# The split tokens and hidden tiles of the experts, stored as interleaved pairs of high and low part

## The chip, the cores and the metric

One core of a Trainium2 chip runs the whole program. The metric is the device time of one execution in microseconds. Five engines work side by side and meet at semaphores: TensorE (PE; its loads of stationary tiles are listed as PEld), VectorE (DVE), ScalarE (ACT), GpSimd (POOL) and SyncE (SP), which issues nearly all transfers.

## The reference, cut to what matters

A bidirectional encoder trunk of two layers on 256 tokens of width 1024. Each layer has four parallel mixers, a gated sum of them, a feed-forward part and a gated embedding. In layer 0 the feed-forward part is one dense SwiGLU; in layer 1 it is a top-2-of-8 mixture of SwiGLU experts of width 3584, and this is what the change touches:

```python
def swiglu(x, w1, w3, w2):
    return (jax.nn.silu(x @ w1) * (x @ w3)) @ w2

def moe_swiglu(x, router, w1, w3, w2):
    logits = jnp.einsum('bsd,de->bse', x, router, preferred_element_type=jnp.float32)
    top_val, top_idx = lax.top_k(logits, TOP_K)
    top_w = jax.nn.softmax(top_val, axis=-1)
    combine = ...                       # (tokens, experts), two entries per token
    for e in range(N_EXPERTS):
        out = out + combine[..., e:e + 1] * swiglu(x, w1[e], w3[e], w2[e])
    return out
```

All inputs and the output are 32-bit floats.

## The kernel before, in words

**Split products.** A product of 32-bit operands is made of three matmuls on operands of type float32r: each operand is stored as a high part (a copy rounded to that type) and a low part (operand minus high part), and `three` (L895 to L899) adds high x high (L897), high x low (L898) and low x high (L899). Its first argument pair holds the stationary tiles, 128 x 128 numbers that are loaded into TensorE before the matmul, and the second pair the moving ones, which stream through it. Every matmul has its own load. In the profile a matmul is written `ps<-moving,stationary`.

**The expert stage.** Each expert is one pass over at most 128 of its tokens (up to 16 passes by the router's counts; 8 here). A pass has 14 chunks of 256 hidden columns. ScalarE makes the high part of each weight unit (`whi`, 128 x 1024, L1563), VectorE the low part (`wlo`, L2128), from a ring of six blocks of 1024 KB that SyncE fills; a chunk takes three blocks, six units. TensorE's chunk is, in order (`step`, L1110):

- 24 up products for the next chunk (`up_unit`, L1079): for each of the 8 slices k of the width, the token tile `xhi`/`xlo[:, k, 0:128]` is stationary and 512 weight columns (w1 and w3 together) move, into one PSUM bank.
- after half of these, two transposes of the present chunk's hidden tile (L1121), which ScalarE copies as high part (`hhi`, L1642) and VectorE turns into the low part (`hlo`, L2277).
- 12 down products (L1137): the hidden tile's two halves `hhi`/`hlo[:, parity, half, 0:128]` are stationary, 512 columns of w2 move.

In chunks 1 to 4 of a pass two scatter products each (L1092) bring the previous pass's results back to the tokens; in chunk 12 the next pass's tokens are gathered (L1073), and ScalarE (L1614) and VectorE (L2254) write them as `xhi` and `xlo`. The order of instructions on every engine is written out by hand. The waits around the changed tiles: TensorE's down products wait for `s_hl`, its up products of a new pass for `s_xl`; ScalarE's writes wait for the transposes and gathers, VectorE's for ScalarE's.

**Where the tiles lie.** `xhi` and `xlo` are 8 x 256 numbers per partition, of which the experts use the first 128 of each 256; `hhi` and `hlo` are 2 x 2 x 256, used likewise. They serve the dense layer and the mixers too, with all 256. In a partition the tensors `xhi`, `xlo`, `hhi`, `hlo`, `whi`, `wlo`, `ring_lo` and `query_key_high_x` start at a multiple of 128 bytes, and so do all their 128-number tiles. `query_key_high` starts 64 bytes past such a multiple.

**Three other places that are spoken of.** In `project` the products `token_major` (L626) have token tiles as stationary operand and 256 weight columns moving; for its last four blocks (`by_parity`) the tile is every second token, `xhi[:, k, tt:256:2]`, so its numbers are 8 bytes apart and start 0 or 4 bytes past the multiple; the first 24 of them have tt = 0 and the next 24 tt = 1. In `query_key` (L670) the stationary tiles are weights: the high part, used for two of the three matmuls, lies in `query_key_high` for the first blocks and then in `query_key_high_x`, the low part in `ring_lo`; 256 tokens move. L1490 on ScalarE copies 128 numbers per partition out of PSUM to every second element of `ybr`, backwards (a step of -2); L1250 copies 256 to neighbouring elements.

Of the kernel before, what the change touches and what calls it, by code (L numbers as in the profile page):

```python
# [29 lines left out]
P = 128  # L30
# [109 lines left out]
AK = SEQ + 2 * P  # L140
BK = TT * SEQ + 2 * P
LINE = 16
DUALS = HP * TT
HEAD_ROWS = ATT_GROUPS * 2 * SEQ


def trunk_program(nc, x, wm, wd, we, wp, pk_in, cst_in, onehot, relb, out):

    ctx = ExitStack()
    with ctx:  # L150
        def sb(name, shape, dt=F32):
            return ctx.enter_context(nc.sbuf_tensor(name, shape, dt))
# [111 lines left out]
        comb = sb("comb", [P, TT, MAX_PASSES + 1])  # L264
        msk = sb("msk", [P, TT, N_EXPERTS])
        pos = sb("pos", [P, TT, MAX_PASSES + 1])


        n_oh = ATT_GROUPS * 2 * SEQ
# [7 lines left out]
        def bank(b, lo=0, n=512):  # L277
            return ps[:, 512 * b + lo:512 * b + lo + n]
# [278 lines left out]
        def _(pe):  # L557
# [343 lines left out]
            def both(hi, lo, *at):  # L901
                return hi[at], lo[at]
# [161 lines left out]
            def experts(passes):  # L1064
# [14 lines left out]
                def up_unit(cc, u, slot, units):  # L1079

                    pe.wait_ge(s_wl, units + (u + 1))
                    for k in (2 * u, 2 * u + 1):
                        col = (k % 2) * 512
                        m = three(bank(cc % 2), both(xhi, xlo, slice(None), k, slice(0, P)),
                                  both(whi, wlo, slice(None), (slot + u) % SLOTS, slice(col, col + 512)),
                                  k == 0, k == KT - 1)
                    m.then_inc(s_wu, 1)
# [18 lines left out]
                with pe.Fori(0, n_p) as q:  # L1106
# [3 lines left out]
                    def step(k, cc, between=None):  # L1110

                        units = u0 + k * 6
                        pe.wait_ge(s_hm, c0 + k)
                        for u in range(4):
                            if cc == EXP_CHUNKS - 1 and u % 2 == 0:
                                pe.wait_ge(s_xl, q * 2 + (6 + u // 2 + 1))
                            up_unit(cc + 1, u, 4, units)
                            if u == 1:
                                pe.wait_ge(s_hm, c0 + k + 1)
                                for half in range(2):  # L1120
                                    m = pe.transpose(bank(2 + cc % 2, half * P, P), gt[:, 0, half * P:half * P + P],  # L1121
                                                     con("ident"))
                                m.then_inc(s_ht, 1)
                        if cc == EXP_CHUNKS - 2:
                            pe.wait_ge(s_stc, q + 2)
                            gather(q + 1)
                        if cc == 0:
                            pe.wait_ge(s_edc, q + 1)
                        if k is cc and 1 <= k <= 4:
                            pe.wait_ge(s_stc, q + 1)  # L1130
                            scatter(q, 2 * k - 2)
                            scatter(q, 2 * k - 1)
                        pe.wait_ge(s_hl, c0 + k + 1)
                        for half in range(2):
                            pe.wait_ge(s_wl, units + (5 + half))
                            for col in range(0, D_MODEL, 512):
                                m = three(bank(4 + col // 512), both(hhi, hlo, slice(None), cc % 2, half, slice(0, P)),  # L1137
                                          both(whi, wlo, slice(None), 2 + half, slice(col, col + 512)),
                                          cc == 0 and half == 0, cc == EXP_CHUNKS - 1 and half == 1)
                            m.then_inc(s_wu, 1)  # L1140
# [81 lines left out]
        def _(act):  # L1222
# [383 lines left out]
            def experts():  # L1606
# [3 lines left out]
                def tokens(n):  # L1610

                    for j in range(2):
                        act.wait_ge(s_xg, n * 2 + (j + 1))
                        act.activation(xhi[:, 4 * j:4 * j + 4, 0:P], bank(6 + j).rearrange("p (c t) -> p c t", c=4),  # L1614
                                       ACT.Copy).then_inc(s_xgc, 1)

                def sums(n):
# [9 lines left out]
                with act.Fori(0, n_p) as q:  # L1627
# [4 lines left out]
                    def chunk(k, cc, j, rr):  # L1632
# [5 lines left out]
                        if cc == EXP_CHUNKS - 2:  # L1638
                            act.wait_ge(s_st, q + 1)
                            act.activation(sca[:, :], bank(6, 0, SEQ), ACT.Copy).then_inc(s_stc, 1)  # L1640
                        act.wait_ge(s_ht, c0 + k + (1 - DENSE_CHUNKS))
                        act.activation(hhi[:, cc % 2, :, 0:P], bank(2 + cc % 2, 0, SEQ).rearrange(  # L1642
                            "p (h t) -> p h t", h=2), ACT.Copy).then_inc(s_hh, 1)
                        if cc == 0:
                            sums(q)
# [80 lines left out]
        def _(dve):  # L1726
# [519 lines left out]
            def experts():  # L2246
# [3 lines left out]
                def tokens(n):  # L2250

                    for j in range(2):
                        dve.wait_ge(s_xgc, n * 2 + (j + 1))
                        dve.tensor_tensor(xlo[:, 4 * j:4 * j + 4, 0:P], bank(6 + j).rearrange("p (c t) -> p c t", c=4),  # L2254
                                          xhi[:, 4 * j:4 * j + 4, 0:P], ALU.subtract).then_inc(s_xl, 1)

                def add(n, m_):

# [9 lines left out]
                with dve.Fori(0, n_p) as q:  # L2268
# [3 lines left out]
                    def chunk(k, cc, j):  # L2272
# [1 line left out]
                        dve.tensor_tensor(hid[:, 0, :], hs[:, 0, :], bank(cc % 2, SEQ, SEQ), ALU.mult).then_inc(s_hm, 1)  # L2274
                        lows(u0 + (k * 6 + 4), 2, 2, j)
                        dve.wait_ge(s_hh, c0 + k + 1)
                        dve.tensor_tensor(hlo[:, cc % 2, :, 0:P], bank(2 + cc % 2, 0, SEQ).rearrange(  # L2277
                            "p (h t) -> p h t", h=2), hhi[:, cc % 2, :, 0:P], ALU.subtract).then_inc(s_hl, 1)
                        if cc == EXP_CHUNKS - 2:
                            dve.wait_ge(s_st, q + 1)  # L2280
                            slots_of(q + 1)
# [282 lines left out]
```

## Time and profile before

| | us |
|---|---|
| three runs | 2147.4, 2148.34, 2148.71 (median 2148.34) |
| the profiled execution, its own time | 2148.84 |
| its span, first to last instruction | 2146.8 |
| TensorE busy | 2116.5 |
| VectorE busy | 1684.4 |
| ScalarE busy | 1323.6 |
| expert loop, from its first to its last chunk (1087.4 to 2092.7) | 1005.3 |

Busy time of TensorE counts overlapping matmuls once, and the end of a matmul is modelled, so what one matmul costs in a stream is read from the distance between starts. A span holds only instructions; the time of an execution is about 2 us more.

### The profile page before, as it was taken

Reading aid. Unit: us, or ns where it says so; the run is one execution under the profiler, and the core shown is the slowest. Engines: PE = TensorE matmul, PEld = TensorE weight load, DVE = VectorE, ACT = ScalarE, POOL = GpSimd, SP = SyncE. Lnnn points to the kernel's source line nnn. Section 1 sums busy time; section 2 is a strip of 40 time slices with the busy share of each in tenths; the row PEclk is TensorE's granted clock in tenths of the full one; section 3 lists DMA queues with packets and bytes.
Section 4 is the critical chain, followed back from the end, with each engine's and each line's share of the span. In section 5 each row is a group of like instructions: output and inputs, shape, how many; then the busy total and the mean of one; then the engine's idle time right before and its main releaser. Section 6 shows DMA issues by size and latency. Waiting matters only on the chain.

```text
span 2146.8 us, 37284 instructions
## 1 busy us (share of the span) xinstructions
PE 2116.5 (99%) x13622; PEld 1905.2 (89%) x13622; DVE 1684.4 (78%) x2373; ACT 1323.6 (62%) x1864; POOL 24.3 (1%) x45
## 2 busy tenths in 40 slices
PE   9999999999999999999999999999999999999997
PEld 8999999999999999999888888888888888888886
DVE  4998866655456898766688888998989899898985
ACT  5545654454435446654467777777777777777773
POOL 0000100000000000100000000000000000000000
PEclk9999999999999999999999999999999999999998
DMA  7534436355345434435379898898999989899981
GB/s 253 188 118 154 143 142 236 138 196 176 137 158 182 164 113 169 147 132 223 138 282 364 341 350 347 345 374 328 358 350 349 347 345 369 339 361 341 351 310 76
DMA packets 74965, 533.19 MB, mean 248 GB/s; under 512 B 8655, under 2 KB 8655, under 8 KB 11000
## 3 DMA queue, kind: packets, MB, share of 16 engines
q1 hardware_dynamic: 72620, 525.04, 64.6%
q0 software_dynamic: 2048, 6.29, 1.6%
q8 instruction: 68, 1.11, 0.2%
q10 hardware_dynamic: 204, 0.54, 0.1%
q14 instruction: 25, 0.20, 0.0%
HBM read 530.74 MB, written 1.10 MB: 248 GB/s over the span
## 4 chain that ended last, share of the span: by engine, by line
PE 95%; DVE 3%; ACT 1%; DMA 1%; issue 0%; SPq 0%; DVEq 0%; ACTq 0%
PE ps L897 28%; PE ps L899 28%; PE ps L898 28%; PE ps L560 4%; PE ps L1092 1%; PE ps L1121 1%; PE ps L851 1%; PE ps L879 1%; PE ps L763 1%; PE ps L866 1%; DMA constants_sb<-constants 0%; DVE rstd L1736 0%; DVE wlo L2128 0%; PE ps L572 0%; DVE xn L1742 0%; DMA ring<-w_ple 0%
## 5 line engine op out<-in xcount | busy, mean ns | idle before, releaser
L2128 DVE TENSOR_TENSOR wlo<-ring,whi 128x1024 fp32r<-128x1024 f32 x746 | 872.8, 1220 | 145.6 <-ACT whi L1563 143.9
L1563 ACT ACTIVATE whi<-ring 128x1024 fp32r<-128x1024 f32 x746 | 749.1, 1054 | 137.9 <-PE ps L899 131.7
L897 PE MATMUL ps<-whi,xhi 128*128 128x512 f32 (+1 forms) x1160 | 434.7, 375 | 1.5 <-DVE xlo L2254 1.5
L899 PE MATMUL ps<-whi,xlo 128*128 128x512 f32 (+1 forms) x1160 | 426.8, 368 | 0.0
L898 PE MATMUL ps<-wlo,xhi 128*128 128x512 f32 x904 | 352.9, 390 | 0.0
L897 PE MATMUL ps<-xhi,whi 128*128 128x256 f32 x960 | 276.6, 288 | 2.5 <-DVE gt L2150 1.4
L898 PE MATMUL ps<-xlo,whi 128*128 128x256 f32 x960 | 273.4, 285 | 0.0
L899 PE MATMUL ps<-xhi,ring_lo 128*128 128x256 f32 x896 | 254.2, 284 | 0.0
L899 PEld LDWEIGHTS ps<-whi,xlo 128*128 128x128 f32 x1160 | 219.2, 189 | 35.8
L897 PEld LDWEIGHTS ps<-whi,xhi 128*128 128x128 f32 x1160 | 219.6, 189 | 33.6 <-DVE xlo L2254 1.9
L899 PE MATMUL ps<-xhi,wlo 128*128 128x256 f32 x704 | 199.2, 283 | 0.0
L898 PEld LDWEIGHTS ps<-wlo,xhi 128*128 128x128 f32 x904 | 170.2, 188 | 32.1
L897 PEld LDWEIGHTS ps<-xhi,whi 128*128 128x128 f32 x960 | 186.1, 194 | 4.7 <-DVE gt L2150 1.6
L898 PEld LDWEIGHTS ps<-xlo,whi 128*128 128x128 f32 x960 | 186.0, 194 | 0.3
L897 PE MATMUL ps<-whi,hhi 128*128 128x512 f32 x448 | 182.7, 408 | 0.0
L899 PE MATMUL ps<-whi,hlo 128*128 128x512 f32 x448 | 175.0, 391 | 0.0
L898 PE MATMUL ps<-wlo,hhi 128*128 128x512 f32 x448 | 174.5, 390 | 0.0
L899 PEld LDWEIGHTS ps<-xhi,ring_lo 128*128 128x128 f32 x896 | 172.4, 192 | 0.0
L1642 ACT ACTIVATE hhi<-ps 128x256 fp32r<-128x256 f32 x112 | 43.0, 384 | 187.9 <-PE ps L1121 187.9
L899 PEld LDWEIGHTS ps<-xhi,wlo 128*128 128x128 f32 x704 | 135.0, 192 | 0.0
L1750 DVE TENSOR_TENSOR ring_lo<-ring,whi 128x1024 fp32r<-128x1024 f32 x68 | 79.8, 1220 | 41.1 <-ACT whi L1242 30.2
L1453 ACT ACTIVATE gs<-ps,half_b_gate 128x256 f32<-128x256 f32 x64 | 30.2, 472 | 122.6 <-PE ps L899 122.6
(307 smaller groups left out, 3832.5 us busy)
## 6 DMA issues: line engine op xcount, KB each, us to landing
ring<-w_experts SPq DMA_DIRECT2D x340, 1024.0 KB, 5.4
ring<-w_mixers SPq DMA_DIRECT2D x114, 1024.0 KB, 4.9
ring<-w_dense SPq DMA_DIRECT2D x33, 1024.0 KB, 4.8
ring<-w_ple SPq DMA_DIRECT2D x10, 1024.0 KB, 4.9
bias<-bias_rows POOLq DMA_DIRECT2D x8, 256.0 KB, 7.1
cvfa<-bias_rows POOLq DMA_DIRECT2D x8, 256.0 KB, 5.2
constants_sb<-constants SPq DMA_DIRECT2D x1, 1048.0 KB, 9.1
h<-x_in SPq DMA_DIRECT2D x1, 1024.0 KB, 4.8
```

What stands on the lines that cost most here:

```text
L560: m = pe.matmul(dst, a, b, start=k == 0, stop=k == len(lhs) - 1)
L763: m = pe.matmul(bank(g, part * P, P), dta[:, tt, at:at + 1].to_broadcast([P, P]), con("from" if d else "upto"), start=True, stop=True)
L851: m = pe.matmul(bank(4 + u, at, n), qk[64 * u:64 * u + 64, g, i, tt * P:tt * P + P], qk[64 * u:64 * u + 64, ATT_GROUPS + g, i, key:key + n ...
L866: m = pe.transpose(bank(u, b * P, P), sa[:, u, b * P:b * P + P], con("ident"))
L897: pe.matmul(dst, lhs[0], rhs[0], start=first, stop=False, skip_group_check=True)
L898: pe.matmul(dst, lhs[0], rhs[1], start=False, stop=False, skip_group_check=True)
L899: return pe.matmul(dst, lhs[1], rhs[0], start=False, stop=last, skip_group_check=True)
L1453: act.activation(gs[:, m_ % 2, :], bank(first_bank + m_ % banks, SEQ, SEQ), ACT.Tanh, bias=half_b[:, bass.ds(b * KT + m_, 1)], scale=0.5). ...
L1563: act.activation(whi[:, slot, :], ring[:, j % RING, lo:lo + UNIT], ACT.Copy).then_inc(s_wh, 1)
L1642: act.activation(hhi[:, cc % 2, :, 0:P], bank(2 + cc % 2, 0, SEQ).rearrange("p (h t) -> p h t", h=2), ACT.Copy).then_inc(s_hh, 1)
L1750: dve.tensor_tensor(ring_lo[:, j % RING, cols], ring[:, j % RING, cols], whi[:, (2 * j + u) % SLOTS, :], ALU.subtract).then_inc(s_ed, 1)
L2128: dve.tensor_tensor(wlo[:, slot, :], ring[:, j % RING, lo:lo + UNIT], whi[:, slot, :], ALU.subtract).then_inc(s_wl, 1)
```

## The change

Two new buffers hold the experts' operands. `x_pair` has, for each slice k, 256 numbers in which high and low part of one token alternate, and 4 more that stay empty, so slices are 1040 bytes apart. `h_pair` is the same for the hidden tiles, with 8 empty numbers after each 256, 1056 bytes apart. Both buffers start at a multiple of 128 bytes. A stationary tile is now every second number, 8 bytes apart; the tiles of x start 0, 16, 32, ... 112 bytes past a multiple of 128, those of h 0, 32, 64 and 96, and the low part of each 4 bytes further. ScalarE and VectorE write with the same step, in the same instructions as before. `xhi`, `xlo`, `hhi` and `hlo` remain for the rest of the program, and the new buffers lie behind all others, so no other address changes. On every engine the order, number and waits of instructions are the same. Lines behind L142 move down by one, those behind L266 by 19.

```diff
--- before.py
+++ after.py
@@ -140,6 +140,7 @@
 AK = SEQ + 2 * P
 BK = TT * SEQ + 2 * P
 LINE = 16
+XSTEP, HSTEP = 4, 8
 DUALS = HP * TT
 HEAD_ROWS = ATT_GROUPS * 2 * SEQ
 
@@ -264,6 +265,24 @@
         comb = sb("comb", [P, TT, MAX_PASSES + 1])
         msk = sb("msk", [P, TT, N_EXPERTS])
         pos = sb("pos", [P, TT, MAX_PASSES + 1])
+        x_pair = sb("x_pair", [P, KT, 2 * P + XSTEP], F32R)
+        h_pair = sb("h_pair", [P, 2, 2, 2 * P + HSTEP], F32R)
+
+        def x_part(part, first, n):
+
+            return x_pair[:, first:first + n, 0:2 * P].rearrange("p c (t s) -> p s c t", s=2)[:, part]
+
+        def x_tile(k):
+
+            return x_part(0, k, 1)[:, 0], x_part(1, k, 1)[:, 0]
+
+        def h_part(part, par_):
+
+            return h_pair[:, par_, :, 0:2 * P].rearrange("p h (t s) -> p s h t", s=2)[:, part]
+
+        def h_tile(par_, half):
+
+            return h_part(0, par_)[:, half], h_part(1, par_)[:, half]
 
 
         n_oh = ATT_GROUPS * 2 * SEQ
@@ -1081,7 +1100,7 @@
                     pe.wait_ge(s_wl, units + (u + 1))
                     for k in (2 * u, 2 * u + 1):
                         col = (k % 2) * 512
-                        m = three(bank(cc % 2), both(xhi, xlo, slice(None), k, slice(0, P)),
+                        m = three(bank(cc % 2), x_tile(k),
                                   both(whi, wlo, slice(None), (slot + u) % SLOTS, slice(col, col + 512)),
                                   k == 0, k == KT - 1)
                     m.then_inc(s_wu, 1)
@@ -1134,7 +1153,7 @@
                         for half in range(2):
                             pe.wait_ge(s_wl, units + (5 + half))
                             for col in range(0, D_MODEL, 512):
-                                m = three(bank(4 + col // 512), both(hhi, hlo, slice(None), cc % 2, half, slice(0, P)),
+                                m = three(bank(4 + col // 512), h_tile(cc % 2, half),
                                           both(whi, wlo, slice(None), 2 + half, slice(col, col + 512)),
                                           cc == 0 and half == 0, cc == EXP_CHUNKS - 1 and half == 1)
                             m.then_inc(s_wu, 1)
@@ -1611,7 +1630,7 @@
 
                     for j in range(2):
                         act.wait_ge(s_xg, n * 2 + (j + 1))
-                        act.activation(xhi[:, 4 * j:4 * j + 4, 0:P], bank(6 + j).rearrange("p (c t) -> p c t", c=4),
+                        act.activation(x_part(0, 4 * j, 4), bank(6 + j).rearrange("p (c t) -> p c t", c=4),
                                        ACT.Copy).then_inc(s_xgc, 1)
 
                 def sums(n):
@@ -1639,7 +1658,7 @@
                             act.wait_ge(s_st, q + 1)
                             act.activation(sca[:, :], bank(6, 0, SEQ), ACT.Copy).then_inc(s_stc, 1)
                         act.wait_ge(s_ht, c0 + k + (1 - DENSE_CHUNKS))
-                        act.activation(hhi[:, cc % 2, :, 0:P], bank(2 + cc % 2, 0, SEQ).rearrange(
+                        act.activation(h_part(0, cc % 2), bank(2 + cc % 2, 0, SEQ).rearrange(
                             "p (h t) -> p h t", h=2), ACT.Copy).then_inc(s_hh, 1)
                         if cc == 0:
                             sums(q)
@@ -2251,8 +2270,8 @@
 
                     for j in range(2):
                         dve.wait_ge(s_xgc, n * 2 + (j + 1))
-                        dve.tensor_tensor(xlo[:, 4 * j:4 * j + 4, 0:P], bank(6 + j).rearrange("p (c t) -> p c t", c=4),
-                                          xhi[:, 4 * j:4 * j + 4, 0:P], ALU.subtract).then_inc(s_xl, 1)
+                        dve.tensor_tensor(x_part(1, 4 * j, 4), bank(6 + j).rearrange("p (c t) -> p c t", c=4),
+                                          x_part(0, 4 * j, 4), ALU.subtract).then_inc(s_xl, 1)
 
                 def add(n, m_):
 
@@ -2274,8 +2293,8 @@
                         dve.tensor_tensor(hid[:, 0, :], hs[:, 0, :], bank(cc % 2, SEQ, SEQ), ALU.mult).then_inc(s_hm, 1)
                         lows(u0 + (k * 6 + 4), 2, 2, j)
                         dve.wait_ge(s_hh, c0 + k + 1)
-                        dve.tensor_tensor(hlo[:, cc % 2, :, 0:P], bank(2 + cc % 2, 0, SEQ).rearrange(
-                            "p (h t) -> p h t", h=2), hhi[:, cc % 2, :, 0:P], ALU.subtract).then_inc(s_hl, 1)
+                        dve.tensor_tensor(h_part(1, cc % 2), bank(2 + cc % 2, 0, SEQ).rearrange(
+                            "p (h t) -> p h t", h=2), h_part(0, cc % 2), ALU.subtract).then_inc(s_hl, 1)
                         if cc == EXP_CHUNKS - 2:
                             dve.wait_ge(s_st, q + 1)
                             slots_of(q + 1)
```

## Rows read from the trace of the kernel before

**Rows 1.** The page's first part: busy us (share of the span), instructions.
```profile
PE 2116.5 (99%) x13622; PEld 1905.2 (89%) x13622; DVE 1684.4 (78%) x2373; ACT 1323.6 (62%) x1864; POOL 24.3 (1%) x45
```
**Rows 2.** The chain that ended last: shares by engine, and by line.
```profile
PE 95%; DVE 3%; ACT 1%; DMA 1%; issue 0%; SPq 0%; DVEq 0%; ACTq 0%
PE ps L897 28%; PE ps L899 28%; PE ps L898 28%; PE ps L560 4%; PE ps L1092 1%; PE ps L1121 1%; PE ps L851 1%; PE ps L879 1%; PE ps L763 1%; PE ps L866 1%; DMA constants_sb<-constants 0%; DVE rstd L1736 0%; DVE wlo L2128 0%; PE ps L572 0%; DVE xn L1742 0%; DMA ring<-w_ple 0%
```
**Rows 3.** Window of the expert loop: busy us by engine, clock, DMA share, GB/s.
```profile
1087.40:2092.70 1005.30, 1005.30 (x4657) 829.98 (x4655) 895.18 (x1008) 755.25 (x936) 0.00 (x0) 1.00 0.91 348
```
**Rows 4.** Order of time, TensorE, one plain chunk: start us, length us, instruction.
```profile
1533.05 0.39 PE L897 MATMUL ps<-whi,hhi 128*128 128x512 f32 x1
...
1538.26 0.40 PE L899 MATMUL ps<-whi,xlo 128*128 128x512 f32 x1
1538.50 0.38 PE L1121 MATMUL ps<-constants_sb,gt 128*128 128x128 f32 x2
...
1538.95 0.39 PE L898 MATMUL ps<-wlo,xhi 128*128 128x512 f32 x1
...
1540.11 0.39 PE L897 MATMUL ps<-whi,xhi 128*128 128x512 f32 x1
...
1541.47 0.39 PE L897 MATMUL ps<-whi,hhi 128*128 128x512 f32 x1
```
**Rows 5.** TensorE's groups by form: count, busy us, mean ns, idle us before.
```profile
L897 PE MATMUL ps<-whi,xhi 128*128 128x512 f32 x904 | 362.3, 401 | 1.5 <-DVE xlo L2254 1.5
L898 PE MATMUL ps<-wlo,xhi 128*128 128x512 f32 x904 | 352.9, 390 | 0.0
...
L897 PE MATMUL ps<-whi,hhi 128*128 128x512 f32 x448 | 182.7, 408 | 0.0
```
**Rows 6.** Order of time, TensorE, value products of layer 0 with every second token.
```profile
102.44 0.28 PE L897 MATMUL ps<-whi,xhi 128*128 128x256 f32 x1
...
105.32 0.28 PE L897 MATMUL ps<-whi,xhi 128*128 128x256 f32 x1
...
108.20 0.28 PE L897 MATMUL ps<-whi,xhi 128*128 128x256 f32 x1
```
**Rows 7.** Order of time, TensorE, query and key products of layer 0.
```profile
143.37 0.28 PE L897 MATMUL ps<-xhi,query_key_high 128*128 128x256 f32 x1
...
153.26 0.28 PE L897 MATMUL ps<-xhi,query_key_high_x 128*128 128x256 f32 x1
...
156.14 0.33 PE L560 MATMUL ps<-ybr,mm 128*128 128x64 f32 x2
```
**Rows 8.** ScalarE's instructions on ybr, then on L1614: ns min/median/max.
```profile
L1250 ACT ACTIVATE ybr<-ps x16: 384/384/388, 67.2 to 731.4; 128x256 f32<-128x256 f32 x16
L1490 ACT ACTIVATE ybr<-ps x16: 275/293/295, 251.4 to 964.0; 128x128 f32<-128x128 f32 x16
...
L1614 ACT ACTIVATE xhi<-ps x18: 576/597/602, 1078.5 to 2081.9; 128x512 fp32r<-128x512 f32 x18
```
**Rows 9.** Order of time, VectorE, a plain chunk; in brackets the wait before.
```profile
1530.91 0.43 DVE L2277 TENSOR_TENSOR hlo<-ps,hhi 128x256 fp32r<-128x256 f32 x1 [0.24 <-ACT hhi L1642]
1531.86 4.63 DVE L2128 TENSOR_TENSOR wlo<-ring,whi 128x1024 fp32r<-128x1024 f32 x4 [0.52 <-ACT whi L1563]
```
**Rows 10.** Order of time, VectorE and TensorE, a pass's new tokens.
```profile
1579.15 1.34 DVE L2254 TENSOR_TENSOR xlo<-ps,xhi 128x512 fp32r<-128x512 f32 x2
...
1581.73 0.39 PE L897 MATMUL ps<-whi,xhi 128*128 128x512 f32 x1
```
**Rows 11.** A ten-microsecond window (columns as rows 3), and the ring's transfers.
```profile
1600.00:1610.00 10.00, 10.00 (x46) 8.25 (x45) 10.00 (x13) 7.70 (x10) 0.00 (x0) 1.00 0.98 402
...
ring<-w_experts SPq DMA_DIRECT2D x340, 1024.0 KB, 5.4
```

## The prediction

> **What bounds the kernel now.** I read the page's first part, then the chain that ended last, then the windows, the groups by form, and last the order of time. TensorE is busy 2116.5 us of 2146.8, VectorE 1684.4 [rows 1]. The chain lies on TensorE for 95% of the span, and 84% of the span is three lines, L897 to L899, the three products of split operands in `three` [rows 2]. The window of the expert loop is the stage that the change touches: 1005.3 us, TensorE busy in all of it, granted clock 1.00 (the upper level, 2.4 GHz), DMA engines 0.91 [rows 3]. So what is left to win there is the distance from one matmul's start to the next, and that stands in the order of time. A plain chunk, from one first down product to the next, is 1541.47 - 1533.05 = 8.42 us. In it 23 undisturbed steps take 1538.26 - 1533.05 = 5.21 us, and the last six 1541.47 - 1540.11 = 1.36 us: 226.7 ns each [rows 4]. The 512 columns alone need 512 / 2.4 = 213.3 ns, so 13.3 ns of each step are not columns.
>
> **How many steps can change.** The loaded (stationary) tiles of the token products are xhi and xlo, of the down products hhi and hlo; each stands in three lines with 904 and 448 matmuls at 512 columns [rows 5]: 3 x 904 + 3 x 448 = 4056. No instruction is added, removed or moved; no semaphore changes; no other buffer's address changes. What changes is where in a partition the 128 loaded numbers lie: before, neighbours, each tile at a multiple of 128 bytes; after, every second number, x tiles at 0, 16, ... 112 bytes past such a multiple (low parts 4 bytes further), h tiles at 0, 32, 64, 96.
>
> **What place costs: the trace has both parts, each at 256 columns.** Step two by itself: the value products take every second token of xhi and xlo as loaded tile, at 0 and 4 bytes past a multiple of 128. The 24 matmuls with tiles at 0 bytes run from 102.44 to 105.32, the 24 with tiles at 4 bytes from there to 108.20 [rows 6]: 2.88 us each, 120.0 ns a step. With neighbouring numbers at multiples of 128 the step is the same: the query and key products that load from query_key_high_x take 156.14 - 153.26 = 2.88 us for 24 [rows 7]. So step two at these places costs and gives nothing. Place by itself: the same routine a moment earlier loads from query_key_high, 64 bytes past a multiple of 128, for two of its three products; the third loads from ring_lo, at a multiple. 84 of them take 153.26 - 143.37 = 9.89 us, 117.7 ns [rows 7]. That is 2.3 ns less per matmul, or 2.3 / (2/3) = 3.4 ns for each tile that lies off the multiple. So while one matmul streams, the load of the next tile slows it, by an amount that hangs on where the two lie.
>
> A rule speaks against this. The Trainium skill ("TensorE: Matmul & The Clock Gate", section "Step-by-step: what each phase is for") says that "Loading the next tile's weights doesn't steal SBUF read bandwidth from the running matmul". By that rule a tile's place cannot change the step, and the change would be worth nothing. The 117.7 beside 120.0 ns [rows 7] doesn't agree with it, at least at 256 columns.
>
> **The sum.** Tiles off a multiple of 128 after the change: x 7 of 8, 2712 x 7/8 = 2373; h 3 of 4 (counting the 4-byte shift as none, since it gave 120.0 above), 1344 x 3/4 = 1008; together 3381. At -3.4 ns: -11.5 us. From both sides the price of one such tile is unknown at 512 columns: at best all 13.3 ns go, at worst the step is the one seen when matmul and load have lost their rhythm. After the two transposes of each chunk the next steps are longer: five take 1540.11 - 1538.95 = 1.16 us, 232 ns, 5.3 over the steady 226.7 [rows 4]. So -13.3 to +5.3 ns a tile, -45 to +18 us. I take -3.4 ns, from the row that is nearest in what it varies, the loaded tile's place; the two ends stay for the range.
>
> The writers of the new tiles: ScalarE and VectorE write every second element, 112 chunks and 9 gathers of tokens. ScalarE's writes with a step of -2 in the trace, 128 elements, took 293 ns against 384 for 256 neighbours [rows 8]; at (597 - 384) / 256 = 0.83 ns an element, from the 512-element copy of tokens [rows 8], 128 neighbours would be 277. So 0 to 16 ns more per 128 elements, and for VectorE, where no row shows it, from nothing to twice the time. Neither is on the chain: the low part of a chunk's hidden tile is ready at 1530.91 + 0.43 = 1531.34 [rows 9], and the first product that it stands in starts after 1533.05 [rows 4], 1.7 us later. Doubled, both engines' writes would take 0.8 us more, still covered. The tightest place is the new tokens of a pass: VectorE done at 1579.15 + 1.34 = 1580.49, TensorE's first product with them at 1581.73 [rows 10], 1.24 us. Doubled writes of both engines would eat that and cost some 0.1 us in each of 8 passes, 1 us. I put 0.
>
> Who is next if TensorE gains: VectorE has 0.24 + 0.52 us of waiting in a plain chunk of 8.42 [rows 9], so it needs 7.66; a chunk without any collision would be 8.42 - 36 x 0.83 x 0.0133 = 8.02. The ring brings three blocks of 1024 KB per chunk, 392 GB/s at 8.02 us; ten-microsecond stretches reach 402 [rows 11], and the loop's mean would rise only from 348 [rows 3] to 364. Neither stops a gain of this size.
>
> The execution that the profile shows took 2148.84 us: a span of 2146.8 and 2.0 around it; the median of the three runs is 2148.34, the same within 0.03%. 2148.8 - 11.5 = 2137.3. Forecast 2137 us.
>
> **Rivals.**
> 1. Nothing changes. A load with step two walks twice as many bytes while it runs, and the only stretch with it shows 120.0 ns at both places tried; if place matters only for neighbours, the step stays 226.7. For it: 120.0 ns with step two [rows 6]. Against: those tiles lie within 4 bytes of the multiple, where place gives nothing either. Time: 2149. The quoted rule gives the same.
> 2. Slower: the rhythm is lost. At 512 columns the steady 226.7 ns is the shortest step that lasts, reached only after five longer ones each time [rows 4]. If tiles that lie differently from one product to the next keep throwing load and stream out of that rhythm, each of the 3381 costs 5.3 ns more: +18 us, 2167. For it: it is the only row of lost rhythm at 512 columns. Against: at 256 columns a changing place made the mean step shorter, not longer. It decides as soon as the mean step in the loop passes 226.7.
> 3. The collision goes wholly. If load and stream only hold each other up where they are at the same place of a 128-byte span at the same time, a load that starts elsewhere with step two may never be: -45 us, 2104. For it: 13.3 of 226.7 ns is there to take, and no other engine stops it. Against: the 117.7 of place alone is still far from the 106.7 ns that 256 columns need.
>
> **Chances.** A change under 0.2% (4.3 us) can't be told from none here. The forecast, a gain of 4 to 25 us, 0.42; rival 3, more than that, 0.16; rival 1 0.17; rival 2 0.25. So faster 0.58, same 0.17, slower 0.25. The range reaches to both bounds, since cases of both signs stand against each other: 2106 to 2168; the forecast's own is 2124 to 2144.
>
> **What would show it.** Right: in the expert loop the steady step falls below 226.7 ns and varies with the tile, a plain chunk is near 8.32 us, and the loop is shorter by the whole gain, with everything before it as it was. The hidden tile's writes stay near 0.38 and 0.43 us, and VectorE's waits shrink. Wrong: steps of 227 throughout (rival 1); steps of 230 and more in the whole chunk, not just after the transposes (rival 2); steps near 214 to 216 (rival 3); or VectorE's subtraction far above 0.43 us with TensorE waiting for it, which would make the writes the price.

## The result, and the profile after

| | before | after |
|---|---|---|
| median of the runs, us | 2148.53 (4 runs) | 2166.45 (4 runs, 2165.41 to 2167.29) |
| ratio after / before | | 1.0084, 95% interval 1.0067 to 1.0102 |
| profiled execution, us | 2148.84 | 2165.41 |
| first to last of the 4056 products of the experts, us | 1081.85 to 2092.65: 1010.80 | 1080.21 to 2108.22: 1028.01 |
| plain chunk, median of 71, us | 8.42 | 8.60 |

The change makes the kernel 0.8% slower. The forecast was 2137 us, faster; what came is the time of rival 2 (2167), at the upper edge of the range.

The page's first part of the kernel after answers to [rows 1], the chain by engine and line to [rows 2] (L916 to L918 are the old L897 to L899):

```profile
PE 2133.3 (99%) x13622; PEld 1932.9 (89%) x13622; DVE 1684.9 (78%) x2373; ACT 1324.7 (61%) x1864; POOL 24.3 (1%) x45
...
PE 95%; DVE 3%; ACT 1%; DMA 1%; issue 0%; SPq 0%; DVEq 0%; ACTq 0%
```

The window from the first to the last product of the experts, in the kernel after and then in the kernel before (us; busy us of PE, PEld, DVE, ACT, POOL; granted clock; DMA share; GB/s):

```profile
1080.21:2108.22 1028.01, 1028.01 (x4679) 862.87 (x4680) 898.59 (x1011) 758.44 (x938) 0.00 (x0) 1.00 0.88 341
```
```profile
1081.85:2092.65 1010.80, 1010.80 (x4679) 834.60 (x4680) 898.12 (x1011) 757.37 (x938) 0.00 (x0) 1.00 0.91 347
```

The same instructions, the same clock, VectorE and ScalarE busy within 1.1 us of before. TensorE is busy all the time and takes 17.21 us longer. Only PE and its loads (PEld, +28 us) have grown. The whole difference therefore lies in the time from one of TensorE's starts to the next. Here is the order of time of one plain chunk after, to be held against [rows 4]:

```profile
1530.40 0.40 PE L916 MATMUL ps<-whi,h_pair 128*128 128x512 f32 x1
...
1533.20 0.39 PE L916 MATMUL ps<-whi,x_pair 128*128 128x512 f32 x1
...
1535.75 0.39 PE L918 MATMUL ps<-whi,x_pair 128*128 128x512 f32 x1
1535.98 0.38 PE L1140 MATMUL ps<-constants_sb,gt 128*128 128x128 f32 x2
...
1536.44 0.39 PE L917 MATMUL ps<-wlo,x_pair 128*128 128x512 f32 x1
...
1538.99 0.39 PE L916 MATMUL ps<-whi,h_pair 128*128 128x512 f32 x1
```

The 12 down products take 1533.20 - 1530.40 = 2.80 us, 233 ns each; the 12 up products after them 1535.98 - 1533.20 = 2.78, 232 ns; the last 11 1538.99 - 1536.44 = 2.55, 232 ns. The settled 226.7 ns of [rows 4] are gone (1% of the token products' steps in the stage last 226 or 227 ns, 75% before); in the plain chunk before, 232 ns were only the five steps behind the transposes. Over the whole stage, taking the times from start to start of neighbouring products of 512 columns: 2431 token products went from a mean of 227.9 to 232.4 ns (+10.8 us), 1287 products of hidden tiles from 228.2 to 233.4 (+6.7). Together 17.5 us, against 17.9 between the medians. The groups by form tell the same [rows 5]: what grew is the modelled length of every product, and the loads beside them (195 ns of one, 188 before; run 2 below has 195 too, runs 3 and 6 have 188 to 189 and lose as much, so the loss does not need the longer load). TensorE's idle time before the new tokens' products, 1.7 us, hardly moved.

```profile
L916 PE MATMUL ps<-whi,x_pair 128*128 128x512 f32 x904 | 366.8, 406 | 1.7 <-DVE x_pair L2273 1.7
L917 PE MATMUL ps<-wlo,x_pair 128*128 128x512 f32 x904 | 355.7, 393 | 0.0
L916 PE MATMUL ps<-whi,h_pair 128*128 128x512 f32 x448 | 185.1, 413 | 0.0
```

The writes are as forecast. ScalarE's copy of a hidden tile takes 402 ns, VectorE's low part the 425 ns it took before, and TensorE waits for neither:

```profile
L1661 ACT ACTIVATE h_pair<-ps 128x256 fp32r<-128x256 f32 x112 | 45.0, 402 | 194.5 <-PE ps L1140 194.5
L2296 DVE TENSOR_TENSOR h_pair<-ps,h_pair 128x256 fp32r<-128x256 f32 x112 | 47.6, 425 | 54.0 <-ACT h_pair L1661 54.0
```

### The profile page after: what moved, and what is told of

Same layout as the page of the kernel before. It is cut to its first block, busy times and chain, and to the rows that moved or that the text cites. A ratio compares the mean times of both kernels' runs of the same rounds, so it can differ in the third digit from the quotient of the medians.

```text
span 2163.3 us, 37284 instructions
## 1 busy us (share of the span) xinstructions
PE 2133.3 (99%) x13622; PEld 1932.9 (89%) x13622; DVE 1684.9 (78%) x2373; ACT 1324.7 (61%) x1864; POOL 24.3 (1%) x45
## 4 chain that ended last, share of the span: by engine, by line
PE 95%; DVE 3%; ACT 1%; DMA 1%; issue 0%; SPq 0%; DVEq 0%; ACTq 0%
PE ps L916 28%; PE ps L918 28%; PE ps L917 28%; PE ps L579 4%; PE ps L1111 1%; PE ps L1140 1%; PE ps L870 1%; PE ps L898 1%; PE ps L782 1%; PE ps L885 1%; DMA constants_sb<-constants 0%; DVE rstd L1755 0%; DVE wlo L2147 0%; PE ps L591 0%; DVE xn L1761 0%; DMA ring<-w_ple 0%
## 5 line engine op out<-in xcount | busy, mean ns | idle before, releaser
L916 PE MATMUL ps<-whi,x_pair 128*128 128x512 f32 x904 | 366.8, 406 | 1.7 <-DVE x_pair L2273 1.7
L918 PE MATMUL ps<-whi,x_pair 128*128 128x512 f32 x904 | 357.7, 396 | 0.0
L917 PE MATMUL ps<-wlo,x_pair 128*128 128x512 f32 x904 | 355.7, 393 | 0.0
L916 PE MATMUL ps<-xhi,whi 128*128 128x256 f32 x960 | 276.0, 288 | 2.6 <-DVE gt L2169 1.4
L918 PE MATMUL ps<-xhi,ring_lo 128*128 128x256 f32 x896 | 253.9, 283 | 0.0
L918 PEld LDWEIGHTS ps<-whi,x_pair 128*128 128x128 f32 x904 | 175.9, 195 | 33.6
L916 PEld LDWEIGHTS ps<-whi,x_pair 128*128 128x128 f32 x904 | 175.8, 194 | 31.7 <-DVE x_pair L2273 2.1
L917 PEld LDWEIGHTS ps<-wlo,x_pair 128*128 128x128 f32 x904 | 176.1, 195 | 31.0
L918 PE MATMUL ps<-xhi,wlo 128*128 128x256 f32 x704 | 199.2, 283 | 0.0
L916 PEld LDWEIGHTS ps<-xhi,whi 128*128 128x128 f32 x960 | 185.6, 193 | 4.7 <-DVE gt L2169 1.6
L916 PE MATMUL ps<-whi,h_pair 128*128 128x512 f32 x448 | 185.1, 413 | 0.0
L917 PE MATMUL ps<-wlo,h_pair 128*128 128x512 f32 x448 | 177.2, 396 | 0.0
L918 PE MATMUL ps<-whi,h_pair 128*128 128x512 f32 x448 | 176.6, 394 | 0.0
L918 PEld LDWEIGHTS ps<-xhi,ring_lo 128*128 128x128 f32 x896 | 171.8, 192 | 0.0
L1661 ACT ACTIVATE h_pair<-ps 128x256 fp32r<-128x256 f32 x112 | 45.0, 402 | 194.5 <-PE ps L1140 194.5
L918 PEld LDWEIGHTS ps<-xhi,wlo 128*128 128x128 f32 x704 | 135.0, 192 | 0.0
```

Source lines behind the costliest of these rows:

```text
L916: pe.matmul(dst, lhs[0], rhs[0], start=first, stop=False, skip_group_check=True)
L917: pe.matmul(dst, lhs[0], rhs[1], start=False, stop=False, skip_group_check=True)
L918: return pe.matmul(dst, lhs[1], rhs[0], start=False, stop=last, skip_group_check=True)
L1661: act.activation(h_part(0, cc % 2), bank(2 + cc % 2, 0, SEQ).rearrange("p (h t) -> p h t", h=2), ACT.Copy).then_inc(s_hh, 1)
```

## The experiments

In the quoted expectations theories A and B of run 1 hold for runs 1 to 3, run 4 names its own, and those of run 8 (R, P, H) hold for runs 9 to 11. "Step one" means neighbouring numbers, "step two" every second one. Runs 1, 4 and 8 are benches of TensorE alone and compute nothing of the reference; the others compute all of it.

**1. Each place alone, on TensorE.** Blocks of 60 matmuls with one load each, from tiles at a set place, 24 to settle and 36 measured.

> Leaves out the whole network: TensorE alone runs 66 blocks of 60 matmuls, each block with one pattern of where the loaded tile and the moving columns lie (step one or two; 0, 16, ... 112 bytes past a multiple of 128), at 512 and at 256 columns; the first 24 of a block settle, the step is read from the last 36. Theory A (the step depends on whether the place changes from one load to the next, not on step two): one place throughout gives 226.7 ns at 512 columns and 120.0 at 256, whatever the place and with step one or two alike; changing places (the eight of the changed kernel, or 64, 64, 0) give 230 to 236 ns at 512 and 117 to 119 at 256. Theory B (step two itself costs at 512 columns): step two gives about 232.6 ns at every place, the eight places with step one stay at 226.7.

Order of time of the bench (one row per block; the first two are 36 measured steps with the tile at 0 bytes and the next block's first 24, the last two the same at 32 bytes):

```profile
19.18 8.32 PE L78 MATMUL ps<-stream_at0b,load_step1at0b 128*128 128x512 f32 x36
27.34 5.60 PE L75 MATMUL ps<-stream_at0b,load_step1at16b 128*128 128x512 f32 x24
...
46.55 8.56 PE L78 MATMUL ps<-stream_at0b,load_step1at32b 128*128 128x512 f32 x36
54.95 5.76 PE L75 MATMUL ps<-stream_at0b,load_step1at48b 128*128 128x512 f32 x24
```

From start to start the place 0 takes (27.34 - 19.18) / 36 = 226.7 ns, the place 32 (54.95 - 46.55) / 36 = 233.3. No other engine works here, so the dearer step needs neither DMA nor writes. At 512 columns nothing is below 226.7; only places 0 and 16 with step one reach it, the rest lie between 229.0 and 234.3, step two at every place between 230.0 and 233.4. At 256 columns the order turns round: 120.0 at place 0, 116.7 to 118.8 at most others. The forecast had carried the sign of 256 columns over to 512.

**2 and 3. Half of the change each.** Run 2 keeps the pairs and drops the empty numbers, so that all tiles start at one place; run 3 keeps the places and stores high and low apart.

```diff
-XSTEP, HSTEP = 4, 8
+XSTEP, HSTEP = 0, 0
```
```diff
-        x_pair = sb("x_pair", [P, KT, 2 * P + XSTEP], F32R)
+        x_pair = sb("x_pair", [P, 2, KT, P + XSTEP], F32R)
...
-            return x_pair[:, first:first + n, 0:2 * P].rearrange("p c (t s) -> p s c t", s=2)[:, part]
+            return x_pair[:, part, first:first + n, 0:P]
```

> The changed kernel without the 4 and 8 empty numbers: pairs with step two, all tiles at 0 or 4 bytes past a multiple of 128. Theory A (changing places cost): steps of 226.7 ns again and 2148 to 2150 us, ratio 1.000. Theory B (step two costs): steps near 232.6 ns and 2166 us, ratio 1.008. Theory C (the writes with step two cost): TensorE waits for x_pair or h_pair, also 2166 us.

> The other half of the change: high and low parts apart, neighbouring numbers (step one), the x tiles at the eight places 0, 16, ... 112 and the h tiles at 0, 32, 64, 96 bytes past a multiple of 128. Theory A: steps of 230 to 236 ns, about 2166 us, ratio 1.008. Theory B: 226.7 ns and 2148 us, ratio 1.000.

Run 2: 2166.03 us, 1.0082 (1.0065 to 1.0098). Run 3: 2165.11, 1.0075 (1.0059 to 1.0092). Each half alone costs all of it. The halves do not add up; each is enough to take away the settled 226.7 ns (means of 233.3 and 233.0 ns for tokens and hidden tiles in run 2, 233.2 and 231.9 in run 3).

**4. Widths.** The bench again, with widths between 192 and 512 columns and some finer places.

> TensorE alone, as in the first bench (each matmul has its own load; 24 to settle, 36 measured): widths of 192, 256, 320, 384, 448 and 512 columns, each with the loaded tile's numbers neighbours at 0, 16, 32 and 64 bytes past a multiple of 128, and every second number at 0; then streams at 16 and 48, and tiles at 4, 8 and 12 bytes, at 256 and 512 columns. The first bench had 120.0, 118.3, 120.1, 117.8 and 120.0 ns at 256 columns and 226.7, 226.7, 233.4, 229.0 and 231.4 at 512. Theory A (the sign belongs to the width: the load's reads fit beside short streams and break the rhythm of long ones): the price of a place moves steadily from -2 to +2 or more ns between 256 and 512, crossing zero near 384 columns. Theory B (the 512-column step at place 0 is one lucky fit): at 320, 384 and 448 columns the places off the multiple are as cheap as place 0 or cheaper, within 1 ns, and 512 alone stands out.

| ns per step, columns | place 0 | 16 | 32 | 64 | step two, 0 |
|---|---|---|---|---|---|
| 192 | 111.6 | 111.7 | 111.7 | 111.7 | 120.1 |
| 256 | 120.0 | 118.2 | 119.9 | 117.7 | 121.2 |
| 320 | 146.7 | 146.7 | 146.7 | 146.7 | 148.0 |
| 384 | 173.3 | 173.3 | 176.7 | 173.3 | 175.0 |
| 448 | 202.7 | 206.7 | 205.3 | 199.9 | 205.0 |
| 512 | 226.7 | 226.7 | 233.4 | 228.8 | 231.4 |

Neither theory as written: no steady drift with the width, and 512 is not a single exception. The price hangs on width and place together. The finer places at 512 columns have a tile 4 bytes past a multiple that costs no more than the one at 0:

```profile
401.14 8.32 PE L72 MATMUL ps<-stream_at0b,load_step1at4b 128*128 128x512 f32 x36
409.30 5.70 PE L69 MATMUL ps<-stream_at0b,load_step1at8b 128*128 128x512 f32 x24
```

(409.30 - 401.14) / 36 = 226.7 ns at 4 bytes; the trace has 230.7 at 8 and 233.3 at 12. At the end of this bench the block of 256 columns at place 64 came a second time, behind another block, and took 113.3 ns instead of 117.7: at one address two rhythms can last.

**5 and 6. One place for all tiles, in the kernel.**

```diff
+PLACE = 4
...
+            at = PLACE + (part * KT + first) * P
+            return x_pair[:, at:at + n * P].rearrange("p (c t) -> p c t", t=P)
```

PLACE counts numbers of 4 bytes: 4 in run 5 (16 bytes), 8 in run 6 (32 bytes); hidden tiles likewise.

> The kernel before with the experts' tiles in buffers of their own, high and low apart, neighbouring numbers, and all tiles 16 bytes past a multiple of 128. If the time follows the bench's price of the place (226.7 ns at 512 columns, as at the multiple): 2148.5 us, 2146 to 2151. If any place off the multiple breaks the rhythm of 512 columns: about 2165 us, as the eight places did.

> The same with all tiles 32 bytes past the multiple. By the bench's price, 233.4 ns, +6.7 ns for 4056 matmuls: +27 us, 2175 us (2171 to 2179), the slowest of all so far. If all places off the multiple cost alike: 2165 to 2166 us, as the eight places (2165.11) and the pairs (2166.03) did. If the tile's place were not the cause, and the new buffers alone were: also 2165.

Place 16: 2162.97 us, 1.0067 (1.0051 to 1.0082). Place 32: 2166.58, 1.0086 (1.0071 to 1.0102). The bench's price of the place failed for 16 bytes (2148.5 was expected from it) and was too high for 32. So "bytes past a multiple of 128" did not look like the right variable.

**7. A version meant to win.** The experts' tiles in buffers of their own at multiples of 128, and `xhi`, `xlo`, `hhi`, `hlo` as a whole 64 bytes further, for the 256-column products that stream them.

```diff
+        pad_a = sb("pad_a", [P, LINE])
         xhi = sb("xhi", [P, KT, SEQ], F32R)
         xlo = sb("xlo", [P, KT, SEQ], F32R)
+        pad_b = sb("pad_b", [P, LINE])
```

> A version that may beat both. The experts' tiles lie in buffers of their own at multiples of 128, neighbouring numbers (226.7 ns at 512 columns); xhi, xlo, hhi and hlo, which the 256-column products of the mixers, the dense layer and the embeddings stream, move as a whole to 64 bytes past a multiple. The bench has 117.8 ns for a load at 0 and a stream at 64, against 120.0 at 0 and 0. Some 5136 such steps x -2.2 = -11.3 us, 384 loads of tokens at 64 another -0.8, 512 query and key steps +0.5 (118.7 against 117.7): -11.6, so 2137 us (2134 to 2142). If place at 256 columns were no gain in the kernel, or these stages wait for weights rather than for TensorE: 2148 to 2150.

2140.01 us, 0.9965 (0.9955 to 0.9976): a gain, but of another make than expected. In the profiled execution, the fastest of eight (2135.03 to 2145.24), the experts began 22.0 us earlier (1059.85), and their stage became 10.7 us longer (1021.46). Order of time of a plain chunk there:

```profile
1533.35 0.39 PE L924 MATMUL ps<-whi,h_pair 128*128 128x512 f32 x1
...
1535.38 0.40 PE L924 MATMUL ps<-whi,h_pair 128*128 128x512 f32 x1
1535.62 0.40 PE L922 MATMUL ps<-whi,x_pair 128*128 128x512 f32 x1
...
1538.41 0.38 PE L1146 MATMUL ps<-constants_sb,gt 128*128 128x128 f32 x2
```

Hidden tiles: nine steps in 2.03 us, 226 ns, the settled rhythm. Token tiles: twelve in 2.79 us, 232 ns, though they too start at a multiple of 128. What may tell the two apart is the distance in bytes from the loaded tile to the stream. By the addresses that the program gives them, `x_pair` lies 128 bytes (mod 256) from `whi` and `wlo`, `h_pair` 0. In the kernel before both were 0.

**8. The distance, measured.** One load buffer and one stream; the distance set in steps of 32 bytes, each block behind 8 matmuls of 128 columns ("free") or behind these and 20 settled steps at distance 0 ("led").

> TensorE alone. In the streams64 run the experts' token tiles stood at multiples of 128 and yet took 232 ns, the hidden tiles 227; token tiles were 384 bytes (mod 512) from the streams, hidden tiles 0; in the kernel before 256 and 0. So here load and stream lie a set distance apart, 0 to 992 bytes in steps of 32, at 512 columns, and 0 to 480 at 256; each block follows 8 matmuls of 128 columns ('free'), or those and then 20 steps at distance 0 ('led'). Theory R (the distance from load to stream counts, not the place past a multiple of 128): 226.7 at distances that are multiples of 256, 229 to 234 at all others, 128 and 384 included, and the same when both lie 128 further. Theory P (the place past a multiple of 128): 226.7 at every multiple of 128. Theory H (a rhythm that history sets): free and led differ, by 3 ns or more, at some of the same distances. Every second number: R 226.7 at 0 and 256; from the pairs that lay 256 apart and took 233, rather 231 or more at all distances.

Windows of 35 steps each (first column from:to, then the length), at 512 columns and a distance of 0, 128 and 256; then 0 and 128 again with load and stream both 128 bytes further; then at 256 columns distance 0, 64 free and 64 led:

```profile
16.77:24.70 7.93, 7.93 (x36) 6.57 (x35) 0.00 (x0) 0.00 (x0) 1.00 0.00 0
153.65:161.79 8.14, 8.14 (x37) 6.60 (x35) 0.00 (x0) 0.00 (x0) 1.00 0.00 0
290.37:298.31 7.94, 7.94 (x37) 6.57 (x35) 0.00 (x0) 0.00 (x0) 1.00 0.00 0
1111.14:1119.08 7.94, 7.94 (x37) 6.57 (x36) 0.00 (x0) 0.00 (x0) 1.00 0.00 0
1140.67:1148.80 8.13, 8.13 (x37) 6.59 (x35) 0.00 (x0) 0.00 (x0) 1.00 0.01 2
1466.07:1470.27 4.20, 4.20 (x38) 4.20 (x37) 0.00 (x0) 0.00 (x0) 1.00 0.00 0
1502.88:1506.85 3.97, 3.97 (x37) 3.97 (x36) 0.00 (x0) 0.00 (x0) 1.00 0.02 4
1513.07:1517.19 4.12, 4.12 (x37) 4.12 (x36) 0.00 (x0) 0.00 (x0) 1.00 0.00 0
```

35 steps in 7.93 or 7.94 us are 226.7 ns each at distances 0 and 256, in 8.13 or 8.14 us 232.4 at 128, and the same when both are moved by 128 bytes. The whole table, from the starts in the trace (load minus stream, mod 256; at 512 columns the four periods up to 992 agree within 0.2 ns):

| distance | 0 | 32 | 64 | 96 | 128 | 160 | 192 | 224 |
|---|---|---|---|---|---|---|---|---|
| 512 columns, step one | 226.7 | 233.3 | 233.3 | 234.3 | 232.4 | 233.3 | 229.0 | 233.3 |
| 512 columns, step two | 233.3 | | 230.0 | | 231.4 | | 233.3 | |
| 256 columns, free | 120.0 | 118.3 | 113.3 | 118.7 | 118.7 | 120.1 | 117.8 | 116.7 |
| 256 columns, led | 120.0 | 118.5 | 117.8 | 117.3 | 118.7 | 119.9 | 113.3 | 116.7 |

Theory R holds at 512 columns, in period and sign; place past a multiple of 128 does not. Of these distances history counts at 256 columns alone, at 64 and 192 (and by 1.4 ns at 96).

Read as distances, by the addresses of their buffers, benches 1 and 4 agree: there place 32 lies at distance 160, 64 at 192, 96 at 224, and step two at place 0 at 128. But between the steps of 32 bytes the price is not smooth. Distance 16 took 226.7 ns, 8 took 230.7 and 80 took 232.0, and the tile at 4 bytes of bench 4 lies at distance 132: 226.7, where 128 takes 232.4 and 140 takes 233.3. With load and stream both at place 16, distance 128 took 233.2. So 0 is the cheapest of the steps of 32, not the only cheap distance, and why the distance matters at all is not shown by any run.

**9 to 11. The distance in the kernel.** Run 9 is run 5 with PLACE = 0: tokens 0 bytes from the streams, hidden tiles 128. Run 10 is run 7 with the tokens' buffer moved by 128 bytes, to distance 0. Run 11 is run 9 with the hidden tiles' buffer moved likewise.

```diff
-        x_pair = sb("x_pair", [P, 2 * KT * P + 32], F32R)
+        pad_e = sb("pad_e", [P, 32])
+        x_pair = sb("x_pair", [P, 2 * KT * P], F32R)
```
```diff
+        pad_h = sb("pad_h", [P, 32])
         h_pair = sb("h_pair", [P, 8 * P + 32], F32R)
```

> The kernel before with the experts' tiles in the new buffers, high and low apart, neighbouring numbers, all at multiples of 128 bytes. Token tiles are then 256 (mod 512) from the streams as before, hidden tiles 384 instead of 0. Theory R: token steps 226.7, hidden steps near 232, +5 ns for 1287 steps: 2155 us (2152 to 2158). Theory P: both 226.7, 2148.5 us. If the new buffers by themselves were the cause: 2163 to 2166, both at 232.

> The streams64 version with its experts' token buffer moved by 128 bytes, so that token tiles are 0 (mod 512) from the streams, as hidden tiles were and are. Theory R: token steps fall from 232.5 to about 228, 2431 steps x -4.5 = -11 us from 2140: 2129 us (2125 to 2134). Theory P: nothing changes, 2140.

> The place0 version with its buffer for hidden tiles moved by 128 bytes, so that these too lie a multiple of 256 bytes from the streams; nothing else differs. Theory R, now with the bench's table (226.7 ns at distance 0 mod 256, 232.4 at 128, 229.0 at 192, 233 to 234 at 32, 64, 96, 160 and 224): hidden steps 233.0 back to 228, as in the kernel before, 1287 steps x -5 = -6.4 us, and the tokens' steps after them settle sooner, 2431 x -1.6 = -3.9: 2147 to 2149 us. Rival: the new buffers cost something by themselves, then it stays above 2152.

Run 9: 2157.57 us, 1.0042 (1.0027 to 1.0057). Run 10: 2129.49, 0.9918 (0.9905 to 0.9932). Run 11: 2148.63, 1.0003 (0.9994 to 1.0013). Each came where the distance put it. Runs 9 and 11 differ in nothing but 128 bytes of padding, and lie 9 us apart. Order of time of a plain chunk of run 9:

```profile
1535.74 0.40 PE L918 MATMUL ps<-whi,h_pair 128*128 128x512 f32 x1
...
1538.54 0.40 PE L918 MATMUL ps<-whi,x_pair 128*128 128x512 f32 x1
...
1540.15 0.39 PE L919 MATMUL ps<-wlo,x_pair 128*128 128x512 f32 x1
...
1541.06 0.40 PE L920 MATMUL ps<-whi,x_pair 128*128 128x512 f32 x1
```

Hidden tiles, distance 128: 2.80 / 12 = 233 ns. Token tiles, distance 0: seven steps in 1.61 us, 230 ns, while the rhythm settles, then four in 0.91, 227 ns. So a product at a bad distance also costs its followers at a good one: the token steps of this run average 229.5, and 227.9 again in run 11. Its window of all experts is that of the kernel before:

```profile
1081.73:2092.53 1010.80, 1010.78 (x4679) 834.60 (x4680) 898.06 (x1011) 757.33 (x938) 0.00 (x0) 1.00 0.92 347
```

Mean steps in the kernels beside the bench, for the distance of each (ns):

| | tokens: distance, bench, kernel | hidden tiles: distance, bench, kernel |
|---|---|---|
| before | 0, 226.7, 227.9 | 0, 226.7, 228.2 |
| run 2, step two | 0, 233.3, 233.3 | 0, 233.3, 233.0 |
| run 6 | 32, 233.3, 233.2 | 160, 233.3, 233.3 |
| run 7 | 128, 232.4, 232.5 | 0, 226.7, 228.8 |
| run 9 | 0, 226.7, 229.5 | 128, 232.4, 233.0 |
| run 11 | 0, 226.7, 227.9 | 0, 226.7, 228.2 |

One entry stays open: run 5 had its tokens at distance 16 and steps of 232.2, 15% of them at 226 or 227. Benches 1 and 4 have 226.7 there, behind a settled block; an unsettled entry at 16 alone was not tried. A block of bench 1 that alternates places 16 and 0 settled at 226.7 within three steps behind one at 231.7. So the distance alone does not foretell run 5.

**12. The best version.** Run 10 with the streams of the dense layer's second products, the low mixer weights and the low half of the mixed rows at distance 64 as well (moved by 128 bytes of padding behind `ring_lo`, and 192 before `mix_low`; the 64 bytes that run 10 has behind `mix_low` and the 128 before `x_pair` fall away, and the experts' tiles stay at distance 0).

```diff
         ring_lo = sb("ring_lo", [P, RING, BLK], F32R)
+        pad_r = sb("pad_r", [P, 2 * LINE])
...
+        pad_c = sb("pad_c", [P, 3 * LINE])
         mlo = sb("mix_low", [P, KT, SEQ], F32R)
```

> The streams64_near version with all 256-column products of the mixers' weights, the dense layer's second products and the low half of the mixed rows brought to a distance of 64 (mod 256) from load to stream, where the bench settled at 113.3 ns (or 117.8, by how it was entered); before, these stood at 192 (118 ns measured). 912 products of the dense hidden tiles 118.0 to 113.3: -4.2 us; 1056 with the low weights 118.5 to 117: -1.6: together 2123.5 us (2121 to 2127). If the other rhythm holds there (117.8): 2129, unchanged. The experts stay at 228.

2117.42 us (five executions, 2116.72 to 2127.96), 0.9874 (0.9856 to 0.9893): faster than both kernels, and 3.6 us below the lower end expected. The dense hidden tiles' products came to 113.3 ns (117.8 in run 10), as expected; 928 products with the low mixer weights did not gain (118.5 to 119.7 in the mean); and 736 products of `xhi` with `wlo`, whose distance was 64 in both, fell unasked from 116.9 to 113.7. Their neighbours' rhythm may have done it; no run shows that. The experts start at 1050.77, 31.1 us earlier than before, and their window is unchanged:

```profile
1050.77:2061.60 1010.83, 1010.83 (x4680) 834.50 (x4680) 898.18 (x1011) 757.38 (x938) 0.00 (x0) 1.00 0.92 347
```

The chain by engine, from the page of the same run: what lies on VectorE has grown from 3% to 7%. That is not yet a price: TensorE is idle for 31.7 us of the span (2114.9 less 2083.2 busy), 30.3 before.

```profile
PE 90%; DVE 7%; ACT 1%; DMA 1%; issue 0%; DVEq 0%; SPq 0%; ACTq 0%
```

## Why the prediction was wrong

**Which stage, how many steps, and where to look: right.** All of the loss lies in the 4056 products of the expert loop; the stretch before it is as it was, within 1.6 us. The 4056 steps, TensorE as the bound and the time between starts as the thing to read held.

**"What place costs": the step that failed.** The prediction took its price from 256 columns, -3.4 ns a tile, and gave it to tiles at 512. Two errors lay in it. First, the variable: [rows 7] was read as "64 bytes past a multiple of 128 against a multiple". By the addresses, `query_key_high` is 192 bytes (mod 256) from the stream `xhi`, `query_key_high_x` and `ring_lo` are 0. The first bench has the same mix at 256 columns, two loads at distance 192 and one at 0: 117.7 ns, and 120.0 for 0 alone, as the rows had it. (All loads at 192 take 117.8 there, so even at 256 columns the gain was not 3.4 ns for each tile off the multiple.) In the kernel before, these tiles and their streams that start at a multiple of 128 also lay 0 (mod 256) apart, so the two readings could not be told apart there. Second, the width: at 256 columns distance 0 is among the dearest states (120.0, others down to 113.3), at 512 nothing is cheaper (226.7, others to 234.3); that same mix of 192 and 0 takes 229.0 at 512. The term -11.5 us was in truth +17.5: not 3381 tiles at -3.4 ns, but nearly all products at +4.5 (tokens) and +5.2 (hidden tiles).

**"Step two costs and gives nothing": wrong at 512 columns.** [rows 6] has 120.0 ns at 256, and the first bench 118.3 to 122.2, but at 512 columns step two takes 230.0 to 233.4 at every distance tried, and run 2, with step two alone, cost the whole 17 us. Rival 1's condition failed here. The 4 bytes between high and low part, counted as none, changed nothing at step two (233.3 ns at distances 0 and 4), though with neighbouring numbers 4 bytes can matter (128 against 132). With TensorE alone at work the same matmul takes 226.7 or 232.4 ns by the loaded tile's distance: load and stream are not independent. The quoted rule of the Trainium skill ("TensorE: Matmul & The Clock Gate", section "Step-by-step: what each phase is for"), read as the prediction read it, allows no such difference; these runs do not agree with it.

**Rival 2 had the sign and the price, and half of the mechanism.** The settled rhythm is indeed lost, but not because tiles lie differently from one product to the next: in run 2 (all at 0 or 4 bytes) and run 6 (all at place 32) the loss is the same. It took 5.3 ns from the five steps after the transposes [rows 4] and 3381 tiles, +18 us; measured were 17.9. Its count was too low and its price a little too high, so that the sum came out this close is partly luck. Its "against" (a changing place shortens the step at 256 columns) was the same wrong transfer. The row that should have weighed more is the only one at 512 columns: in it the steps sit at 226.7 ns or above, so the rows showed that something can be lost there, and nothing to gain.

**Rival 3** needed steps of 214 to 216 ns; no state of any bench at 512 columns is below 226.7. Its 2104 us lay 2 us outside the range, which was said to reach both bounds.

**Writers: right; next bounds: not put to the test,** since no step of the experts became shorter. ScalarE's writes of a hidden tile grew by 18 ns (0 to 16 was estimated for half as many numbers) and those of tokens from 596 to 655, VectorE's by none, and TensorE's wait for new tokens is 1.7 us in all, 1.5 before.

## What to carry to other kernels

In a stream of matmuls that each load a tile, the step depends on the tile's layout and on its distance from the moving operand in the partition, with a period of 256 bytes here, and the best of the distances in steps of 32 bytes differs by width: 0 at 512 columns with neighbouring numbers, 64 or 192 at 256. Finer distances have to be measured one by one (132 is as cheap as 0 at 512, 128 is not). Padding of 64 to 192 bytes before some buffers, with buffers of their own for the experts' tiles, was worth 31 us of 2148 here at the same number of instructions. A price read at one width is not one for another: measure it at the width that the change touches. And count on a step shorter than the stage has ever shown only where a bench has shown it: at 512 columns none was there, at 256 the kernel's 117 to 120 ns came to 113.3.

## What was not expected of the hardware

- The step behaves like a lasting rhythm rather than a sum of costs. At 256 columns and distance 64 the same stream lasted at 113.3 ns or at 117.8, by what ran before it; in the kernel, products at distance 0 needed about seven steps to reach 226.7 behind products at distance 128.
- The floor over the bare columns, 13.3 ns at 512, is not fixed: at 256 columns 113.3 is 6.6 ns over 106.7.
- Smaller loads did not help at 512 columns: with 64 or 32 columns loaded at distance 0 the first bench has 230.0 and 231.7 ns, more than with 128 (226.7); at 256 columns both have 113.3.
- At 192 columns and step one the place does not show (111.6 to 111.7 ns), and 128 columns took the same 111.7.
